# TensorE's order around two normalisations: projections ahead of the transposes of the normed outputs

## What is computed

```python
for l in range(DEPTH):                        # DEPTH = 2
    u_lat = modulate(x, sh1, sc1)
    u_ctx = modulate(xc, ch1, cs1)
    y_ctx, y_lat = token_mixers(u_ctx @ w_in[l], u_lat @ w_in[l], P, l, lower_bounds[l], rope, not last)
    x = layer_norm(DEEPNORM_ALPHA * x + g1 * (y_lat @ w_out[l]), ln1_w[l], ln1_b[l])
    x = layer_norm(DEEPNORM_ALPHA * x + g2 * peer_ffn(modulate(x, sh2, sc2), P), ln2_w[l], ln2_b[l])
    # in the first layer the context stream xc goes the same way
```

```python
def rwkv7_finish(o, p, P):
    oc = o - o.mean(-1, keepdims=True)
    y = oc * lax.rsqrt((oc * oc).mean(-1, keepdims=True) + RWKV_GN_EPS)
    ...                                       # y * ln_w + ln_b, plus a bonus
    return (y + bonus.reshape(bsz, t, A_WIDTH)) * p['g']

def finish(o):                                # of the attention
    y = rms_norm(o, P['diff_subln_w']) * (1.0 - lam_init)
```

## Time and profile before

| | us |
|---|---|
| median of 3 runs | 6001.18 (5999.1 to 6006.35) |
| the profiled execution | 6002.42 |
| its span in the trace | 6000.6 |
| PE busy in it | 5152.3 (86%) |
| DVE busy | 3722.8 (62%) |
| ACT busy | 1465.9 (24%) |
| POOL busy | 1470.7 (25%) |
| PE's mean granted clock | 0.893 |

### The profile page before, as it was taken

The page is one execution under the profiler, slowest core; times in us unless marked ns, Lnnn a source line. Parts: engine busy times, 40 slices in busy tenths (PEclk is TensorE's granted clock), DMA queues, the critical chain, the costliest instruction groups (busy, mean ns, idle before and its releaser), DMA issues.

```text
span 6000.6 us, 63022 instructions
## 1 busy us (share of the span) xinstructions
PE 5152.3 (86%) x22127; PEld 3419.4 (57%) x22127; DVE 3722.8 (62%) x8344; ACT 1465.9 (24%) x3650; POOL 1470.7 (25%) x1540
## 2 busy tenths in 40 slices
PE   8899887888776899999999589978798657999997
PEld 3588553667643455555555368845475545666664
DVE  1544371756966797877665455434465786786565
ACT  1111031322566221112111211002222283121111
POOL 0000000000126555545553000000000055344552
PEclk9899988589887999999999789989758757999998
DMA  6000001004358999999997100000002258999996
GB/s 227 21 12 8 21 5 56 1 22 151 124 195 326 366 415 411 400 399 409 401 409 302 62 11 8 8 25 15 35 1 85 105 207 346 416 420 419 416 416 266
DMA packets 294042, 1191.31 MB, mean 199 GB/s; under 512 B 24800, under 2 KB 106976, under 8 KB 208224
## 3 DMA queue, kind: packets, MB, share of 16 engines
q0 software_dynamic: 92160, 671.13, 27.3%
q1 hardware_dynamic: 195808, 460.83, 20.8%
q10 hardware_dynamic: 5760, 55.33, 2.3%
HBM read 1135.81 MB, written 51.38 MB: 198 GB/s over the span
## 4 chain that ended last, share of the span: by engine, by line
PE 62%; DVE 19%; DMA 10%; ACT 4%; issue 2%; POOL 2%; ACTq 0%; DVEq 0%; SPq 0%; POOLq 0%
PE psum L537 62%; DMA arena<-in_ut 6%; DVE arena L1476 3%; DMA arena<-gate_blocks 2%; DVE arena L1631 1%; DVE arena L1822 1%; DVE x_tokens L1476 1%; DVE arena L1897 1%; DMA arena<-in_uv,arena 1%; DVE arena L1485 1%; DMA x_tokens<-in_uv,arena 1%; DVE arena L1629 1%; DVE u_features L1482 1%; DVE y_features L1726 1%; ACT y_features L1169 1%
## 5 line engine op out<-in xcount | busy, mean ns | idle before, releaser
L537 PE MATMUL psum<-arena 128*128 128x64 f32 (+4 forms) x8128 | 1439.3, 352 | 31.2 <-DVE arena L1822 24.2
L537 PE MATMUL psum<-u_features,weight_ring 128*128 128x256 f32 (+2 forms) x4672 | 1351.6, 441 | 31.2 <-ACT arena L1198 17.5
L537 PEld LDWEIGHTS psum<-arena 128*128 128x128 f32 (+1 forms) x8128 | 1032.5, 212 | 399.3 <-issue 309.5
L537 PEld LDWEIGHTS psum<-u_features,weight_ring 128*128 128x128 f32 x4672 | 883.6, 193 | 401.1 <-issue 193.5
L1454 POOL TENSOR_TENSOR arena<-consts 128x1 f32<-128x1 f32 x640 | 335.2, 524 | 1231.3 <-DVE y_features L1726 1098.8
L537 PE MATMUL psum<-u_features,arena 128*128 128x384 f32 (+1 forms) x2048 | 581.5, 438 | 41.3 <-DMA arena<-in_ut 37.2
L537 PE MATMUL psum<-weight_ring,consts 128*128 128x512 f32 x1280 | 570.4, 592 | 2.3 <-DVE consts L1713 1.9
L537 PE MATMUL psum<-arena,y_features 128*128 128x128 f32 (+1 forms) x1632 | 375.3, 387 | 192.1 <-ACT y_features L1171 87.3
L537 PEld LDWEIGHTS psum<-u_features,arena 128*128 128x128 f32 x2048 | 392.3, 192 | 253.7 <-issue 56.3
L1455 POOL DMA_INDIRECT arena<-in_uv,arena x350 | 486.8, 1391 | 99.3 <-POOL arena L1454 94.0
L1087 ACT ACTIVATE arena<-psum 128x512 f32<-128x512 f32 (+5 forms) x388 | 237.6, 612 | 1095.3 <-PE psum L537 864.0
(11 more groups left out here) (208 smaller groups left out, 5361.4 us busy)
## 6 DMA issues: line engine op xcount, KB each, us to landing
weight_ring<-in_ws SPq DMA_DIRECT2D x242, 512.0 KB, 3.6
weight_ring<-in_ut SPq DMA_DIRECT2D x128, 512.0 KB, 10.6
weight_ring<-in_uv SPq DMA_DIRECT2D x128, 512.0 KB, 13.0
arena<-in_ut SPq DMA_DIRECT2D x128, 512.0 KB, 16.2
arena<-in_uv SPq DMA_DIRECT2D x128, 512.0 KB, 10.5
gate_blocks<-arena ACTq DMA_DIRECT2D x20, 2048.0 KB, 7.6
arena<-gate_blocks SPq DMA_DIRECT2D x32, 768.0 KB, 17.8
arena<-gate_blocks SPq DMA_DIRECT2D x32, 512.0 KB, 27.8
```

Source lines behind the costliest of these rows:

```text
L537: return pe.matmul(o, w, x, start=first, stop=last, skip_group_check=True)
```

## The change

The change reorders PE's stream at two places in each layer, and ACT's copies with it; DVE's stream differs in one operand.

At the RWKV output, "rwkv g" is written to banks 4 to 6 instead of 0 to 2. The two attention pieces follow it directly. The wait for "rwkv y" stands behind them, since the values are written to banks 0 to 5, of which 4 and 5 hold "rwkv g". The transposes of RO move behind the first two rotated matmuls, after a wait for "attn v kept", and the wait for "rwkv y features" to where "attn v kept" was awaited.

At the attention's output, the first four HGRN pieces stand directly behind the last job. Then come a wait for ACT's copy of the fourth (the transposes use the same banks), the wait for "attn y", the transposes, a wait for the second feature copy, the two other HGRN pieces, and the wait for the fourth feature copy.

```diff
-                    ins = mm(PS[:, t * 256:(t + 1) * 256], lo_[64:128, t * P:(t + 1) * P], SW[64:128, 0:256])
+                    ins = mm(PS[:, 2048 + t * 256:2048 + (t + 1) * 256], lo_[64:128, t * P:(t + 1) * P], SW[64:128, 0:256])
                 done(ins, "rwkv g", l)
-                pe.wait_ge(*at("rwkv y", l))
-                for b in range(2):
-                    for t in tiles(l):
-                        ins = pe.transpose(turned(2 * b, t), RO[:, t * 256 + b * P:t * 256 + (b + 1) * P], ident)
-                done(ins, "rwkv y turned", l)
-                pe.wait_ge(*at("rwkv y features", l))
-
                 project(l, "attn", AQK, NT)
                 pe.wait_ge(*at("attn copied", l, AQK - 1))
+                pe.wait_ge(*at("rwkv y", l))
                 project_tokens("attn", xt, range(NT), "attn v", l)
                 for n in range(8):
 
+                    if n == 2:
+                        pe.wait_ge(*at("attn v kept", l))
+                        for b in range(2):
+                            for t in tiles(l):
+                                ins = pe.transpose(turned(2 * b, t), RO[:, t * 256 + b * P:t * 256 + (b + 1) * P], ident)
+                        done(ins, "rwkv y turned", l)
...
                 pe.wait_ge(*at("rope", l, 7))
-                pe.wait_ge(*at("attn v kept", l))
+                pe.wait_ge(*at("rwkv y features", l))
...
+                project(l, "hgrn", BH)
+                pe.wait_ge(*at("hgrn copied", l, BH - 1))
                 pe.wait_ge(*at("attn y", l))
                 for h in range(BH):
                     for t in tiles(l):
                         ins = pe.transpose(turned(2 * h, t), OA[:, t * 512 + h * P:t * 512 + (h + 1) * P], ident)
                     done(ins, "attn y turned", l, h)
+                pe.wait_ge(*at("attn y features", l, 1))
+                project(l, "hgrn", HF, BH)
                 pe.wait_ge(*at("attn y features", l, BH - 1))
-
-                project(l, "hgrn", HF)
                 pe.wait_ge(*at("hgrn copied", l, HF - 1))
```

More of the change, by code:

```diff
@@ L1285, in _ @@
                         copy(q["u"], bank(b0 + 1, 0, 256), "rwkv U kept", l, i, d)
[L1286 to L1289, removed]
                 for c in range(NT, AQK):
@@ L1295, in _ @@
                 copy(VA, PS[:, 0:NT * 512], "attn v kept", l)
+                act.wait_ge(*at("rwkv y turned", l))
+                lo = 0 if l + 1 < DEPTH else CTX
+                copy(yt(0, lo), pair(0, lo))
+                copy(yt(1, lo), pair(2, lo), "rwkv y features", l)
                 jobs = [(t, h) for t in ts for h in range(BH)]
@@ L1313, in _ @@
                         copy(PT_[(n - 1) % 2][:, 0:keys], PS[:, 2048:2048 + keys], "attn aT", l, n - 1)
+                for c in range(BH):
+                    act.wait_ge(*at("hgrn projected", l, c))
+                    copy(AR[:, c * T:(c + 1) * T], pair(2 * (c % 2)), "hgrn copied", l, c)
                 for h in range(BH):
@@ L1316, in _ @@
                     copy(yt(2 + h, lo), pair(2 * h, lo), "attn y features", l, h)
-                for c in range(HF):
+                for c in range(BH, HF):
                     act.wait_ge(*at("hgrn projected", l, c))
@@ L1869, in _ @@
                 dve.wait_ge(*at("rwkv g", l))
-                tt(RO, RO, PS[:, 0:NT * 256], ALU.mult, "rwkv y", l)
+                tt(RO, RO, PS[:, 2048:2048 + NT * 256], ALU.mult, "rwkv y", l)
                 for n in range(8):
```

## The result

The changed kernel takes 5903.68 us (median of 4 runs, 5893.52 to 5929.98) against 6000.78 us of the kernel before (4 runs, 5999.1 to 6006.35): a ratio of 0.984, 95% interval 0.981 to 0.988. The forecast was 5918 us with a range of 5909 to 5930. The profiled execution took 5900.72 us with a span of 5898.9 us, 101.7 us less than that of before.

What follows compares the result with a forecast made beforehand. PE was taken to bound most stages, with real idle time under DVE's normalisations at both places. Shifts of 23.1 + 23.0 + 22.3 + 15.7 = 84.1 us, off the profiled 6002.42 us, gave 5918 us, range 5909 to 5930.

Steps and rivals of the forecast that it cites:

- A: RWKV output: attention pieces directly behind "rwkv g" let the values start 23.1 us earlier in layer 0, 23.0 in layer 1.
- B, layer 0: Attention's output, layer 0: four HGRN pieces under DVE's normalisation give a shift of 22.3 us (21.8 to 22.9).
- B, layer 1: Attention's output, layer 1: HGRN pieces moved ahead of the transposes give a shift of 15.7 us (15.3 to 15.9).
- The attention jobs meet another clock: Rival: layer 0's eight short context jobs run at the upper clock, 4 us less in all, 5914 us; chance 0.07.
- The 1.7 us for a cold start at B: Attention's output: 1.7 us less shift in each layer if the moved HGRN pieces start at the low clock.
- the rope: Attention ropes on DVE: RO's transposes between rotated matmuls cost 0 to 0.3 us, taken as 0; 2.5 together at worst.
- the weights: SP's queue: the next four weight pieces are already in the ring, so nothing waits for weights at either place.
- The shift should be kept to the end: Behind both places everything waits by semaphore, so the whole 84.1 us should last to the kernel's end.
- The prediction's own sign: Each layer's stretch from the end of its HGRN values to the layer's end would be as before.
- Jobs at the better level: Rival case: layer 0's short attention context jobs at the upper clock, total 5908 to 5914 us; chance 0.07.
- rival of a low clock through the moved pieces: Both places: six moved pieces a layer at half speed cost 124.4 us in all, giving 6043 us; chance 0.02.
- a slower DVE chain: RWKV output: normalisation half as slow again beside busy PE loses 7.9 us a layer, 5930 to 5940 us; chance 0.05.

Runs made afterwards that it cites:

- e1: Only the move at the RWKV output, made to the kernel before, with the attention's output left as it was; 5956.2 us, ratio 0.990.
- e6: The changed kernel without the idle matmuls ahead of each level of the HGRN scan; 5845.5 us, ratio 0.973.

## Why the forecast was right and where it failed

**What bounds the stage, and the sum: right.** The moves were priced at 84.1 us and measured 83.4 (three traces each), 83.3 and 83.1 with other keepers, and 89.3 with the later scan. The terms were less exact than the sum, which is so close in part by luck: their errors cancel. *A* was given 46.1 us and brought 43.8: the two pieces took 23.3 to 23.4 us in four of the six places of the three traces, above the upper bound of 22.45, and 22.2 and 22.0 in the other two, because the clock had already fallen inside "rwkv g". By the Trainium skill, "TensorE: Matmul & The Clock Gate", section "What's actually happening", the instant differs from run to run; the traces agree (22.00 to 23.44 us), and the middle between a warm and a cold start was the wrong pick where the trace showed the fall. *B, layer 0*: 22.3 forecast, 21.6 measured; *B, layer 1*: 15.7 forecast, 18.0 measured. Of that, 2.5 us lie in the attention jobs and not under the normalisation: 1.2 in the first jobs, where a group of 12 products took 1.52 us instead of 2.75, and 1.3 at the last job's end, where the transposes now ran at the upper level (from them to the last product 4.09 us before, 2.75 after). e1, without the second move, has the same 2.5 us. So the rival "The attention jobs meet another clock" came true in part, in layer 1 and not in the context jobs it named. The 1.7 us for a cold start at B stands on no row: the rows gave 22.45 - 20.91 = 1.5 us, and the pieces at the RWKV output paid up to 2.5. Transposes of 3.0 and 2.0 us measured 2.84 and 1.97; the rope lost 0.1 us where 0 was taken; the normalisation stayed hidden, DVE's chain of 22.7 us is 22.7 again, and the weights were there.

**"The shift should be kept to the end": the step that failed.** It was argued from the semaphores, which is enough for work whose duration is fixed. The prediction's own sign for it failed: the interval from the end of the HGRN values to the end of the layer was to be as before. The HGRN scan behind both places has no fixed duration: by when it meets the low clock it takes 227 to 248 us in the traces of the kernel before and 223 to 242 in those of the changed one. Its change was left at nothing in the sum; in the first pair of traces it was 18.4 us, over three traces each 12.9. I had looked at the clock only inside the moved stretches, and read "Jobs at the better level" as the only place with such a choice, where each HGRN scan offers up to 25 us against the 4 named there. In the trace of before it could be seen: equal chunks of 30.1 and 36.9 us beside each other.

**The range: too narrow for that reason.** It took the spread of the three runs shown, 7 us, as that of the kernel. Further runs of the unchanged kernel lay between 5992 and 6028 us. Two scans with some 20 us of play each, rather than 7 us in all, would have asked for a range some 25 us wide on either side. The rival of a low clock through the moved pieces did not occur (41.45 us for four pieces in the first trace, 42.2 and 42.3 in layer 0 of the two others); nor did a slower DVE chain.

**What stays open.** The medians of the changed kernel and of the one before differ by 97.1 us as they are, and by 92.6, 100.9 and 103.3 us with two keepers, with none and with the later scan: always more than 83.4. The lists of chunks repeat often (247.6 us in layer 1 in three traces of before and in e1, never in the changed kernel), which speaks for a scan that, with the change, starts at a better place against the clock on average. Three traces each put that at 13 us, but they do not pin it down, and another edit ahead of the scan may undo it. It is argued and not shown, and it can't be all: without keepers the scans of the two traces differ by only 4.3 us, and the medians still by 100.9.

## What to carry to other kernels

Work that does not depend on a normalisation can be put under it, and its price follows from one timeline: idle time, minus the copies and transposes that stay. Before a sum is carried to the end of a program, look for stages behind the edit in which the same instructions take different times at different granted clocks; their spread belongs into the range, even where the few runs at hand agree. Where PE with its idle matmuls fills the path at the low clock, try to run without them: here that was worth some 58 us, more than half of what the change itself gave.

## What the hardware showed that I had not expected

PE was busy for 35.46 of 36.90 us of a chunk by the trace and was still granted a mean of 0.54 of its clock. With a second idle matmul of 128 x 128 per level the mean was 0.89 and the chunk took 30.7 us instead of 36.9, although that added work; without any, the clock stood at 0.55 to 0.66 in the middle chunks of e6, and they took 28.8 to 30.4 us. And the same kernel, executed again, had chunks of 36.9, 35.3, 30.1, 36.9 and 35.3 us where it had had 30.1, 36.9, 35.3, 30.2 and 21.9.
